# Latent and block heads: scaled probabilities, and two heads' values in one step, written transposed

## The reference, cut to what matters

```
latent heads (6, called "mla"):   p = softmax(q k^T * 96**-0.5, causal)            a = p v   [256 x 384]
block heads  (6, called "mo"):    p = softmax(q k^T / 8 + slope * distance, ...)   b = p v   [256 x 384]
dilated heads (12, called "di"):  the same with other masks, three groups combined  c         [256 x 256]
merged = gate0 * (a @ w_br_mla) + gate1 * (b @ w_br_moba) + gate2 * (c @ w_br_dil)
y = merged @ w_out
```

## Time and profile before

| | |
|---|---|
| three runs | 2876.13 us median, 2874.94 to 2878.03 |
| the profiled execution | 2875.68 us, of which the span in the trace is 2873.8 us |
| PE matmul | 2831.5 us busy, 99% of the span |
| PE weight loads | 2515.9 us, 88% |
| DVE | 1817.9 us, 63% |
| ACT | 1485.6 us, 52% |
| POOL | 231.6 us, 8% |
| the chain that ended last | PE 83%, DVE 9%, ACT 4% |
| transfers | 504.11 MB at 174 GB/s read, 49% of the 16 engines' time |

### The profile page before, as it was taken

The page is one execution under the profiler, slowest core; times in us unless marked ns, Lnnn a source line. Parts: engine busy times, 40 slices in busy tenths (PEclk is TensorE's granted clock), DMA queues, the critical chain, the costliest instruction groups (busy, mean ns, idle before and its releaser), DMA issues.

```text
span 2873.8 us, 45049 instructions
## 1 busy us (share of the span) xinstructions
PE 2831.5 (99%) x18180; PEld 2515.9 (88%) x18180; DVE 1817.9 (63%) x2698; ACT 1485.6 (52%) x2304; POOL 231.6 (8%) x187
## 2 busy tenths in 40 slices
PE   8999999999999999999999999999999999999998
PEld 8989878989989879989988887899799888878897
DVE  5646665646655675645568778665555587786654
ACT  5445555445445555444446567544344465675442
POOL 0010001010010011010014100010100131000100
PEclk9999999999999999999999999999999999999999
DMA  6544444555544445555555444555555454444553
GB/s 237 180 168 162 145 154 176 178 180 191 199 163 141 147 153 197 193 193 194 189 178 178 144 154 147 205 198 183 184 197 191 171 194 138 163 148 181 204 201 117
DMA packets 74780, 504.11 MB, mean 175 GB/s; under 512 B 8752, under 2 KB 10448, under 8 KB 18768
## 3 DMA queue, kind: packets, MB, share of 16 engines
q1 hardware_dynamic: 74576, 501.24, 49.1%
HBM read 500.12 MB, written 1.08 MB: 174 GB/s over the span
## 4 chain that ended last, share of the span: by engine, by line
PE 83%; DVE 9%; ACT 4%; issue 1%; POOL 1%; DMA 0%; SPq 0%; DVEq 0%; ACTq 0%
PE ps L1485 41%; PE ps L1503 37%; PE ps L1524 2%; DVE wlo L1945 2%; DVE conv L2240 1%; DVE pr L2342 1%; ACT whi L1681 1%; POOL wlo L2402 1%; PE ps L1611 1%; ACT pr L1910 1%; DVE sm L2343 1%; DVE pr L2339 1%; ACT pr L1916 1%; ACT pr L1908 1%; PE ps L1609 1%
## 5 line engine op out<-in xcount | busy, mean ns | idle before, releaser
L1681 ACT ACTIVATE whi<-raw 128x1024 fp32r<-128x1024 f32 (+3 forms) x938 | 976.9, 1043 | 878.3 <-PE ps L1485 443.6
L1945 DVE TENSOR_TENSOR wlo<-raw,whi 128x1024 fp32r<-128x1024 f32 (+2 forms) x894 | 1076.1, 1216 | 301.4 <-ACT whi L1681 300.4
L1503 PE MATMUL ps<-xT_hi,whi 128*128 128x256 f32 x3296 | 926.9, 281 | 1.0 <-DVE v_mla L2167 1.0
L1503 PE MATMUL ps<-xT_lo,whi 128*128 128x256 f32 x3296 | 920.4, 279 | 0.0
L1503 PE MATMUL ps<-xT_hi,wlo 128*128 128x256 f32 x3296 | 919.8, 279 | 0.0
L1503 PEld LDWEIGHTS ps<-xT_hi,whi 128*128 128x128 f32 x3296 | 619.4, 188 | 7.9 <-issue 6.9
L1503 PEld LDWEIGHTS ps<-xT_lo,whi 128*128 128x128 f32 x3296 | 619.6, 188 | 0.6
L1503 PEld LDWEIGHTS ps<-xT_hi,wlo 128*128 128x128 f32 x3296 | 619.4, 188 | 0.0
L1485 PE MATMUL ps<-whi,xT_hi 128*128 128x512 f32 (+2 forms) x1152 | 462.7, 402 | 6.8 <-DVE wlo L1945 2.4
L1485 PE MATMUL ps<-whi,xT_lo 128*128 128x512 f32 (+2 forms) x1152 | 449.6, 390 | 0.0
L1485 PE MATMUL ps<-wlo,xT_hi 128*128 128x512 f32 (+2 forms) x1152 | 449.3, 390 | 0.0
(11 more groups left out here) (315 smaller groups left out, 2482.2 us busy)
## 6 DMA issues: line engine op xcount, KB each, us to landing
raw<-in_w SPq DMA_DIRECT2D x436, 1024.0 KB, 4.8
vr<-in_vrows SPq DMA_DIRECT2D x19, 512.0 KB, 5.7
raw<-in_w SPq DMA_DIRECT2D x12, 768.0 KB, 4.2
raw<-in_w SPq DMA_DIRECT2D x10, 896.0 KB, 4.5
sums<-scratch SPq DMA_DIRECT2D x8, 512.0 KB, 4.6
raw<-in_w SPq DMA_DIRECT2D x4, 832.0 KB, 4.5
raw<-in_w SPq DMA_DIRECT2D x4, 576.0 KB, 3.7
x<-in_x SPq DMA_DIRECT2D x2, 512.0 KB, 5.3
```

Of the source, the lines that this page charges most:

```text
L1503: made = e.matmul(out, ws[:, o:o + 128], xs[:, kt, :], start=kt == 0 and n == 0 and c % 2 == 0, stop=kt == job.nk - 1 and n == 2, skip_gro ...
L1681: e.activation(out, raw, ACT.Copy).then_inc(*mark("hi", i))
L1945: e.tensor_tensor(out, raw, hi.bitcast(F32), sub).then_inc(*mark("lo", i))
```

## The change

For the latent and the block heads (12 heads in each of two layers, 24 in all; not the dilated heads):

- The division moves to the probabilities. A new step `norm_probs` on DVE takes the reciprocal of the sums and scales the probabilities in place, 128 and 256 columns. The transposes of `turn_probs` wait for it instead of for the exponentials.
- `values` and `normed` go. Every second turn, `values_pair` makes the values of two heads with `values_T`, and `halve_o` writes ACT's rounded half and DVE's rest of the pair straight into `oTa` or `oTb`.
- `to_T` of `o_mla` and `to_T_steps` of `o_moba` go, and with them the two arrays.
- Within a turn, the values now stand before `norm_probs` and `turn_probs` in the list. In both functions `scores` stays ahead of them.
- `halve_o` gets a width `n` (1 for the new calls, 2 for the old one).

```diff
-    def normed(self, key, view, den, n, ps, after):
-        self.do("normed", key, view, den, n, ps, self.stat(2), after)
-        self.aux.put(ps, ("copy_v", "o", *key))
-        return ("copy_v", "o", *key)
+    def norm_probs(self, key, p, after, den):
+        self.do("norm_probs", key, p, after, den, self.stat(2))
+        return ("vec", "norm", *key)
+
+    def values_pair(self, keys, qs, vs, pts, oT, k, after):
+        ps, free = self.aux.get()
+        self.do("values_T", keys[0], keys, qs, vs, ps, free, after)
+        for q in qs:
+            pts.put(q, ("att", "v", *keys[0]))
+        key = (oT.name, oT.gen, k)
+        self.do("halve_o", key, ps[:, 0:256].unsqueeze(1), ("att", "v", *keys[0]), oT, k, 1, oT.free)
+        oT.ready[k] = [("xlo", *key)] * 2
+        self.aux.put(ps, ("xlo", *key))
...
@@ heads: block and dilated heads, turn s, after the scores of head s
-                if 0 <= s - 2 < len(items):
-                    kind, h = items[s - 2]
-                    p, after, den = probs[s - 2]
-                    turned[s - 2] = self.turn_probs((kind, l, h), p, after, prs, pts)
                 if 0 <= s - 3 < len(items):
                     kind, h = items[s - 3]
                     key = (kind, l, h)
...
-                    if kind == "mo":
-                        v = [v1[:, t, 64 * h:64 * h + 64] for t in (0, 1)]
-                        ps = self.values(key, turned[s - 3], v, 64, pts, (v_there[0, 0], v_there[0, 1]))
-                        res["mo"] = self.normed(key, m["o_moba"][:, :, 64 * h:64 * h + 64], den, 64, ps,
-                                                ("exp", *key))
-                    else:
+                    if kind == "mo" and h % 2:
+                        v = [[v1[:, t, 64 * i:64 * i + 64] for t in (0, 1)] for i in (h - 1, h)]
+                        self.values_pair([("mo", l, h - 1), key], [turned[s - 4], turned[s - 3]], v, pts, oTb, h // 2,
+                                         (v_there[0, 0], v_there[0, 1]))
+                    elif kind == "di":
...
+                if 0 <= s - 2 < len(items):
+                    kind, h = items[s - 2]
+                    p, after, den = probs[s - 2]
+                    if kind == "mo":
+                        after = self.norm_probs((kind, l, h), p, after, den)
+                    turned[s - 2] = self.turn_probs((kind, l, h), p, after, prs, pts)
...
@@ mla_heads: turn s, after the scores of head s-1
+                if 0 <= s - 4 < 6 and s % 2:
+                    h = s - 4
+                    v = [[m["v_mla"][:, t, 64 * i:64 * i + 64] for t in (0, 1)] for i in (h - 1, h)]
+                    self.values_pair([("mla", l, h - 1), ("mla", l, h)], [pT[h - 1], pT[h]], v, pts, oTa, h // 2,
+                                     tuple(("copy_v", "ukv", l, j, t) for j in (0, 1) for t in (0, 1)))
                 if 0 <= s - 3 < 6:
                     h = s - 3
                     p, after, den = probs[h]
+                    after = self.norm_probs(("mla", l, h), p, after, den)
                     pT[h] = self.turn_probs(("mla", l, h), p, after, prs, pts)
-                if 0 <= s - 4 < 6:
-                    h = s - 4
-                    v = [m["v_mla"][:, t, 64 * h:64 * h + 64] for t in (0, 1)]
-                    ps = self.values(("mla", l, h), pT[h], v, 64, pts,
-                                     (("copy_v", "ukv", l, h // 3, 0), ("copy_v", "ukv", l, h // 3, 1)))
-                    res["mla"] = self.normed(("mla", l, h), m["o_mla"][:, :, 64 * h:64 * h + 64], probs[h][2], 64,
-                                             ps, ("exp", "mla", l, h))
...
-            self.to_T([m["o_mla"][:, t, :] for t in (0, 1)], (res["mla"],), 3, oTa)
+            oTa.gen += 1
...
-        second = self.to_T_steps([m["o_moba"][:, t, :] for t in (0, 1)], (res["mo"],), 3, oTb)
...
-                      [m["xn"][:, t, :] for t in (0, 1)], self.xn_free, second, third, 1.0)
+                      [m["xn"][:, t, :] for t in (0, 1)], self.xn_free, iter(()), third, 1.0)
...
@@ DVE's program
-    def normed(key, view, den, n, ps, r, after):
+    def norm_probs(key, p, after, den, r):
         dve.wait_ge(*at(*after))
         step(e.reciprocal(r, den))
-        dve.wait_ge(*at("att", "v", *key))
-        e.tensor_tensor(view, ps[:, 0:2 * n].rearrange("p (t d) -> p t d", t=2), bc(r, n), mul
-                        ).then_inc(*mark("copy_v", "o", *key))
+        e.tensor_scalar(p[:, 0:128], p[:, 0:128], r[:, 0:1], None, mul)
+        e.tensor_scalar(p[:, 128:384], p[:, 128:384], r[:, 1:2], None, mul).then_inc(*mark("vec", "norm", *key))
```

More of the change, by code:

```diff
@@ L281, in memory @@
             sbuf("v1", [128, 2, 1152], F32, ph)
-            sbuf("o_mla", [128, 2, 384], F32, ph)
-            sbuf("o_moba", [128, 2, 384], F32, ph)
             sbuf("o_dil3", [128, 2, 768], F32, ph)
@@ L842, in heads @@
                     key = (kind, l, h)
-                    den = probs[s - 3][2]
-                    if kind == "mo":
-                        v = [v1[:, t, 64 * h:64 * h + 64] for t in (0, 1)]
-                        ps = self.values(key, turned[s - 3], v, 64, pts, (v_there[0, 0], v_there[0, 1]))
-                        res["mo"] = self.normed(key, m["o_moba"][:, :, 64 * h:64 * h + 64], den, 64, ps,
-                                                ("exp", *key))
-                    else:
+                    if kind == "mo" and h % 2:
[3 more added lines that the diff above has]
+                    elif kind == "di":
                         v = [v1[:, t, 384 + 64 * h:448 + 64 * h] for t in (0, 1)]
@@ L857, in heads @@
                     yield
+            oTb.gen += 1
             w = self.stat(24)
@@ L1322, in third @@
                 key = (oT.name, oT.gen, k)
-                self.do("halve_o", key, oc[:, k:k + 2, :], ("copy_v", "o", "c", l, 2 * k + 2), oT, k, oT.free)
+                self.do("halve_o", key, oc[:, k:k + 2, :], ("copy_v", "o", "c", l, 2 * k + 2), oT, k, 2, oT.free)
                 oT.ready[k] = oT.ready[k + 1] = [("xlo", *key)] * 2
@@ L1711, in turn_h, with halve_o @@
                      ).then_inc(*mark("xhi", "h", s, c))
-    def halve_o(key, src, there, xt, k, xfree):
+    def halve_o(key, src, there, xt, k, n, xfree):
         act.wait_ge(*at(*there))
@@ L1716, in halve_o @@
             act.wait_ge(*at(*f))
-        e.activation(xt.H[:, k:k + 2, :], src, ACT.Copy).then_inc(*mark("xhi", *key))
+        e.activation(xt.H[:, k:k + n, :], src, ACT.Copy).then_inc(*mark("xhi", *key))
     def scale_row(s, row, rstd, ps, free, row_free):
@@ L2047, in halve_h, with halve_o @@
                         ).then_inc(*mark("xlo", "h", s, c))
-    def halve_o(key, src, there, xt, k, xfree):
+    def halve_o(key, src, there, xt, k, n, xfree):
         dve.wait_ge(*at("xhi", *key))
-        e.tensor_tensor(xt.L[:, k:k + 2, :], src, xt.H[:, k:k + 2, :].bitcast(F32), sub).then_inc(*mark("xlo", *key))
+        e.tensor_tensor(xt.L[:, k:k + n, :], src, xt.H[:, k:k + n, :].bitcast(F32), sub).then_inc(*mark("xlo", *key))
     def add_x(s, t, ns, banks, half, tok, x_free, in_psum):
@@ L2359, in vector_program @@
         "add_x": add_x, "scores": scores,
-        "normed": normed, "o_out": o_out, "dil_weights": dil_weights, "dil_sum": dil_sum, "latents": latents,
+        "norm_probs": norm_probs, "o_out": o_out, "dil_weights": dil_weights, "dil_sum": dil_sum, "latents": latents,
         "bank_out": bank_out, "uq_out": uq_out, "ukv_out": ukv_out, "merge": merge, "scalars": scalars,
```

## The result

| | before | after |
|---|---|---|
| median of the runs | 2876.2 us | 2907.6 us |
| lowest to highest | 2874.9 to 2878.0 us | 2904.7 to 2908.9 us |
| profiled execution: time, span | 2875.7, 2873.8 us | 2907.2, 2905.4 us |
| mean granted clock | 0.998 | 0.995 |

The change makes the kernel slower: the ratio is 1.0108, with a 95% interval of 1.0095 to 1.012, and 31.4 us are lost. The forecast was 2901.4 us with a range of 2895.5 to 2910. The sign and the range hold, and so does the mechanism of the waits; the middle is 6.2 us too low.

A forecast was written before the change was run, and what follows sets the result against it. The prediction took PE, busy for 99% of the span, to bound the kernel. From 2875.68 us it added 33.3 us of new waits and took off 7.6 us of shed PE work: 2901.4 us, range 2895.5 to 2910.

The forecast's parts named there:

- PE has no slack: Block heads of layer 0: PE busy 45.00 of 45.00 us, so work shed or waits added count one for one.
- The wait, term by term: PE before the transposes: DVE's scores, norm_probs 0.73 us and handover 0.15; without a pair 2.21 us latent, 2.30 block.
- the row of 512 columns from SBUF: Earlier trace's scaling of 0.48 us, used to cost the scalings of 128 and 256 columns at 0.28 and 0.35 us.
- the bound of 0.93 for norm_probs: Upper bound in us for norm_probs on DVE, if every column costs the full 1.04 ns; 0.73 was taken.
- Which turns wait: Latent turns 3 to 7 and block turns 2, 4, 5 and 6 wait; 16.6 us per layer, 33.3 in two.
- The gains: PE sheds 4.6 us by values made in pairs and 3.0 us by transposes of o_mla and o_moba, together 7.6.
- The side-by-side rule: Values of a pair: matmuls in different column groups run together, for 4.8 us less; the trace was held to disagree.
- What was costed at nothing: DVE's added scalings, the pair's PSUM bank, the dilated heads' new order, oTa and oTb, SP's and POOL's queues: no cost.
- a sign that it is wrong: The prediction is wrong if, among other signs, the clock falls below 1.00 in the heads.
- this rival: Waits in the heads also lower PE's clock: 8 falls of 1.6 us, 13 us on top, 2914 us; chance 0.10.
- DVE is ahead: norm_probs is done before PE reaches the transposes, so no waits and only the 7.6 us count: 2868.1 us; chance 0.05.
- Only the scaling is waited for: The turn's scores are already done, so 16 waits of 0.88 us before the transposes: 2882.2 us; chance 0.03.
- the pair is not cheaper: Two heads' values still cost PE 1.18 us, so 4.6 us come back: 2906.0 us; chance 0.04.

The follow-up runs named there:

- norm_first: The changed kernel with norm_probs moved to the head of the turn, ahead of the scores; 2868.1 us, ratio 0.9974 to the kernel before.
- pairs_alone: The changed kernel without norm_probs, so the division is left out and the result is not the reference's; 2866.8 us, ratio 0.9968 to the kernel before.
- norm_first_singles: The kernel before with norm_probs added at the head of the turn, single heads' values copied out undivided, no pairs, transposes kept; 2879.6 us, ratio 1.0011.
- change_filled: The changed kernel with idle matmuls on PE ahead of the wait for the scaled probabilities; 2901.8 us, ratio 1.0088 to the kernel before.
- norm_before_halves: The changed kernel with norm_probs still behind the scores but ahead of the pair's subtract on DVE; 2900.7 us, ratio 1.0087 to the kernel before.
- norm_alone: The kernel before with norm_probs added behind the scores, single heads' values copied out undivided, no pairs, transposes kept; 2926.2 us, ratio 1.0173.
- change_longer_norm: The changed kernel with two more DVE passes over the probabilities behind the two scalings; 2933.9 us, ratio 1.020 to the kernel before.
- norm_alone_filled: The kernel before with norm_probs added behind the scores and idle matmuls on PE ahead of the waits; 2914.3 us, ratio 1.0131.

## Why the prediction was right, and by how much it missed

*PE has no slack, and DVE's part of a turn begins when PE's is nearly over.* Right, and it decided the sign. norm_first, where DVE does the scaling before PE's part of the turn, lost nothing.

*The wait, term by term.* The scores on DVE: 1.12 us from their start to the reciprocal (906.28 to 907.40) against 1.13. The scalings: 0.29 and 0.35 us against 0.28 and 0.35, so the row of 512 columns from SBUF was the right kin, and the bound of 0.93 for norm_probs was too wide. Handover to PE: 0.06 us (the scaling ends at 908.14, PE starts at 908.20) against the 0.15 taken; this is the one term that was off, and its lower bound was nearer. From the moment at which PE would have begun the transposes a latent turn without a pair cost about 2.13 us (2.21 forecast), one with a pair 1.67 (1.80), block turn 2 2.31 (2.30), block turns 4 and 6 1.75 (1.84), block turn 5 0.46 (0.4). That is 16.0 us a layer and 32.0 in all, for 33.3.

*Which turns wait.* All nine a layer as listed, in both layers, and no others.

*The gains.* 7.6 us by the sum, 8.7 by pairs_alone, within its interval. The pair takes 0.80 us.

*The side-by-side rule, read wrongly.* The prediction held that the four matmuls of 256 columns in the earlier trace rows, 0.12 us each, run one after the other. They do not. What one such float32 matmul takes by itself stands in the scores of the same kernel before: two of 256 columns, of one head, from 267.10 to the 267.53 of the earlier trace rows, 0.22 each. The timeline of PE in pairs_alone, asked for the 0.02 us from 272.30 to 272.32 alone, shows two matmuls of the pair already begun:

```profile
267.10 0.60 PE L1611 MATMUL ps<-qkT 96*128 96x256 f32 x2
272.31 0.44 PE L1640 MATMUL ps<-pt,v_mla 128*64 128x256 f32 x2
```

Four one after the other would take 0.86 us; they take 0.48, since each two of them, one of each head, run together. So the rule of the Trainium skill (TensorE: Matmul & The Clock Gate, Part 3: Packing small matmuls), that matmuls whose outputs start in different column groups run at the same time, holds here. The row that the sum used already had it in its 0.80 us. The price was right, and there never was another 4.8 us to be had.

*What was costed at nothing.* The scalings and the halves on DVE, nearly rightly: pairs_alone and norm_first are 1.2 us apart, and in norm_first_singles the scalings come to 3.7.

*The term that was put at nothing.* 32.0 - 7.6 is 24.4, and the run lost 31.4. The missing 7 us are the clock: 6.9 in the heads, and up to 3.4 at the branches, as upper bounds. The fall in the heads is, in the prediction's own words, a sign that it is wrong, and on this step it was: the forecast was for waits at the full clock. The range held the result because its upper end made room for the mild end of this rival; the 2901.4 and its 0.78 did not. The rival had 8 falls of 1.6 us and a chance of 0.10, and the reason against it was that each wait stands alone between large matmuls. That reason was wrong: in the change the clock was low behind four of the eight waits of 1.96 us or more that have no pair, each of them alone, and behind none of the eight of 1.6 to 1.7 us. With 4 falls of about 1.5 us the forecast would have been 2907. change_filled shows the two parts apart: 2901.8 us with the clock kept, 2907.6 without. So the likeliest case should have been waits with some falls, and neither none nor half of them. The Trainium skill (TensorE: Matmul & The Clock Gate, Why this matters for your kernels) warns that idle gaps between bursts of matmuls put the clock back, but for longer gaps than these. Here the measurement decides: single gaps of 1.96 to 2.24 us were enough in four of eight places.

*The rivals.* "DVE is ahead" is not what the change does, but it is what norm_first does, at 2868.1 us for the 2868.1 worked out. "Only the scaling is waited for" fell with the timelines above, and "the pair is not cheaper" with pairs_alone.

## What to carry to other kernels

When a step is put between two engines that hand work to and fro, look where it stands in the queue of the engine that makes it. Behind an instruction that waits for the other engine's work of the same turn, it turns a pipeline into a ladder, and the cost is the whole rest of that queue, not the step (0.73 us of step cost 2.1 us a turn here). One place earlier, where its inputs have long been ready, the same instructions cost next to nothing: 2907.6 us became 2868.1 by moving one call in each of the two functions. And an in-order PE that stands for about 2 us pays twice when its clock falls behind it, so count the waits first and then ask how many of them are long.

## What the runs showed of the hardware

A single wait of about 2 us between large matmuls is sometimes followed by the lower level of the clock, mostly for some 3 us and in a few places for twice that, and sometimes not. Over the heads, behind waits of 1.95 to 2.3 us the clock was low in 4 of 8 places in the change, 4 of 8 in norm_before_halves and 10 of 14 in norm_alone; behind waits of 1.15 to 1.7 us it was low in none of 15 in these three; behind 2.4 to 3.0 us in 9 of 16 in change_longer_norm. The same wait in the other layer could go the other way (latent turn 3 of the change, 1.96 us in both: 1.00 in layer 0, 0.75 in layer 1), so length is not all of it; what else decides was not tried. The wait for xn at the branches, 2.2 to 2.5 us, goes either way too: in the kernel before the clock fell behind it in layer 1 alone, in the change in both layers. Filling the waits with matmuls whose result nobody uses kept the clock at 1.00 in every one of them, in two kernels, and won 5.9 and 11.9 us.

Time won on PE's clock is not won in full: where DVE is next in line PE stands longer one turn later, 1.4 us in change_filled and 4.0 in norm_alone_filled.

Two float32 matmuls of 256 columns, one for each of two heads, with outputs in rows 0 to 63 and 64 to 127, start together: four of them took 0.48 us, where two of one head's scores took 0.43.
